# Encoder layer on one core: three of the four late modulation vectors summed on VectorE, ScalarE and GpSimd; Fourier mixer with folded columns

## What is computed

```python
mod = jax.nn.silu(c) @ w_ada[l] + b_ada[l]                    # c: one vector per sequence, w_ada 1024 x 6144
sh_m, sc_m, gt_m, sh_f, sc_f, gt_f = jnp.split(mod, N_MOD, axis=-1)
h = modulate(x, g_mix[l], sh_m, sc_m)
x = x + gt_m[:, None, :] * token_mixer(h, w_in[l], ...)
h = modulate(x, g_ffn[l], sh_f, sc_f)
x = x + gt_f[:, None, :] * expert_choice_moe(h, ...)          # 16 experts, each token list of 128 + 64

# token_mixer: z = h @ w_in, split in zb, zc, za (384 each), zf (256), zu, zv (384 each)
def fourier_mixer(zf):
    f = zf.reshape(b, s, FOURIER_GROUPS, HEAD_DIM)
    y = jnp.real(jnp.fft.fft2(f, axes=(1, 3), norm='ortho'))  # over the sequence and over the head
```

## Time and profile before

| | |
|---|---|
| median of 3 runs | 1515.03 us (1514.19 to 1516.32) |
| the profiled execution's own time | 1515.15 us |
| its span | 1513.3 us |
| TensorE busy (matmuls) | 1436.5 us, 95% |
| VectorE, ScalarE, GpSimd busy | 1032.3, 775.0, 158.1 us |
| mean granted TensorE clock | 0.982 |
| ada steps of the prompt | 72.1 to 271.9 us |
| prompt's sequence transform | 271.9 to 285.8 us |

### The profile page before, as it was taken

The page is one execution under the profiler, slowest core; times in us unless marked ns, Lnnn a source line. Parts: engine busy times, 40 slices in busy tenths (PEclk is TensorE's granted clock), DMA queues, the critical chain, the costliest instruction groups (busy, mean ns, idle before and its releaser), DMA issues.

```text
span 1513.3 us, 22821 instructions
## 1 busy us (share of the span) xinstructions
PE 1436.5 (95%) x8639; PEld 1277.9 (84%) x8639; DVE 1032.3 (68%) x1449; ACT 775.0 (51%) x1020; POOL 158.1 (10%) x129
## 2 busy tenths in 40 slices
PE   2999999999999986999999999999999999999992
PEld 1787777887788866999999999999999999999992
DVE  3422533676769877777777777777777767777776
ACT  4422121523542324666656666666666666666564
POOL 2000000000000002021021021022022022022010
PEclk9999999999999997999999999999999999999996
DMA  9334344554242364687788788788778778778786
GB/s 331 107 113 126 115 150 150 188 180 181 90 120 57 133 240 156 219 275 245 244 265 244 257 257 249 256 260 251 254 245 266 254 243 267 253 241 263 250 280 241
DMA packets 217941, 322.20 MB, mean 213 GB/s; under 512 B 7452, under 2 KB 174440, under 8 KB 217896
## 3 DMA queue, kind: packets, MB, share of 16 engines
q1 hardware_dynamic: 208760, 294.70, 57.8%
q0 software_dynamic: 8064, 26.30, 7.4%
q10 hardware_dynamic: 1072, 0.59, 0.1%
HBM read 290.07 MB, written 31.49 MB: 212 GB/s over the span
## 4 chain that ended last, share of the span: by engine, by line
PE 83%; DVE 8%; ACT 3%; DMA 2%; SPq 1%; issue 1%; POOL 0%; POOLq 0%; DVEq 0%; ACTq 0%
PE ps L1589 25%; PE ps L1237 24%; PE ps L1587 10%; PE ps L1610 4%; PE ps L1602 4%; PE ps L1611 4%; PE ps L1603 4%; PE ps L1606 4%; PE ps L1592 1%; DVE wlo L2172 1%; PE ps L1578 1%; DVE idxu L2040 1%; SPq L631 1%; DVE vals L2038 1%; DVE aff L2041 1%
## 5 line engine op out<-in xcount | busy, mean ns | idle before, releaser
L1589 PE MATMUL ps<-xT,whi 128*128 128x384 f32 x2048 | 576.6, 356 | 1.6 <-DVE xT L2288 1.6
L2172 DVE TENSOR_TENSOR wlo<-raw,whi 128x2048 fp32r<-128x2048 f32 x191 | 435.3, 2292 | 193.1 <-ACT whi L1134 193.1
L1587 PE MATMUL ps<-xT,wlo 128*128 128x192 f32 x1792 | 455.3, 254 | 0.0
L1589 PEld LDWEIGHTS ps<-xT,whi 128*128 128x128 f32 x2048 | 367.9, 189 | 2.4 <-issue 1.9
L1134 ACT ACTIVATE whi<-raw 128x2048 fp32r<-128x2048 f32 x192 | 362.4, 1906 | 0.0
L1587 PEld LDWEIGHTS ps<-xT,wlo 128*128 128x128 f32 x1792 | 342.5, 191 | 0.0
L1237 PE MATMUL ps<-hT,wring 128*128 128x512 f32 x1224 | 289.7, 395 | 5.7 <-DVE hT L1720 5.7
L1237 PEld LDWEIGHTS ps<-hT,wring 128*128 128x128 f32 x1224 | 229.4, 190 | 58.8 <-DVE hT L1720 6.3
L1171 ACT ACTIVATE gu_l<-ps 128x384 f32<-128x384 f32 x128 | 62.9, 491 | 152.4 <-PE ps L1589 152.4
L1237 PE MATMUL ps<-wo,Yhl 128*128 128x512 f32 x576 | 135.5, 393 | 2.4 <-DVE Yhl L1862 1.0
L1237 PEld LDWEIGHTS ps<-wo,Yhl 128*128 128x128 f32 x576 | 106.9, 188 | 25.3 <-issue 2.1
(11 more groups left out here) (236 smaller groups left out, 1551.9 us busy)
## 6 DMA issues: line engine op xcount, KB each, us to landing
raw<-in_w_gate SPq DMA_DIRECT2D x64, 1024.0 KB, 4.8
raw<-in_w_up SPq DMA_DIRECT2D x64, 1024.0 KB, 5.6
raw<-in_w_down SPq DMA_DIRECT2D x64, 1024.0 KB, 5.5
wraw<-in_w_in SPq DMA_DIRECT2D x34, 512.0 KB, 6.0
wraw<-in_w_ada SPq DMA_DIRECT2D x32, 512.0 KB, 4.6
ada_w<-in_w_ada SPq DMA_DIRECT2D x16, 512.0 KB, 11.3
acc_d<-x SPq DMA_DIRECT2D x12, 512.0 KB, 2.7
h_d<-h SPq DMA_DIRECT2D x12, 512.0 KB, 3.9
```

Of the source, the lines that this page charges most:

```text
L1587: pe.matmul(out[:, 0:CAP], wlo[:, slot, w], xT[:, k, 0:CAP], start=False, stop=False, skip_group_check=True)
L1589: mm = pe.matmul(out[:, 0:2 * CAP], whi[:, slot, w], xT[:, k, :], start=k == 0, stop=k == KB - 1, skip_group_check=True)
L2172: dve.tensor_tensor(wlo[:, j % SPL, :], raw[:, j % RAW, :], whi[:, j % SPL, :].bitcast(F32), ALU.subtract).then_inc(w_split, 1)
```

## The change

Four things are changed.

1. **ada parts 0, 1 and 2** (24 of 32 pieces) leave TensorE. For the prompt VectorE forms a running sum, piece times silu(c) per row plus the sum so far (`ada_prompt`). For the sample ScalarE scales the piece into one buffer `ada_part`, and GpSimd adds it to its sum (a copy for the first piece of a part); ScalarE waits for GpSimd before it writes the buffer again. A piece is free when both VectorE and ScalarE are done with it. A new step "sum", one block after a part's last piece, lets TensorE add the 128 partitions of both sums (`ada_sums`, 8 matmuls as wide as those of one ada pair). Part 3 stays as it was.
2. **Fourier columns folded.** VectorE folds the positions n and s-n (`fold`, in the step of zv0), so the head transform needs 16 matmuls of 128 columns (and two of the middle position) in place of 16 (prompt) or 8 (sample) of 256, and the sequence transform half its matmuls and half its constants: two pieces instead of four (prompt), one instead of two (sample). The sums and differences after the head transform go away.
3. The step ab0 comes after zv1 instead of before it, in both sequences.
4. w_out blocks 1 and 2 are loaded behind za2 and zb2. The bias rows of the late parts come one part at a time, because sums and bias lie in space of Y that zb1 and later blocks write.

```diff
-WO_AHEAD = {("zb", 0): 5, ("zb", 1): 6, ("zc", 2): 7}
+AB_JOBS = (2, 1)
+N_SUMMED = (N_ADA - 1) * KB
+WO_AHEAD = {("zb", 0): 5, ("zb", 1): 6, ("zc", 2): 7, ("za", 2): 1, ("zb", 2): 2}
...
-    order = ["zf0", "zf1", "zv0", "ab0", "zv1", "vt0", "zv2", "vt1", "zu0", "vt2", "zu1", "zu2", "zc0", "sv0", "za0", "zb0",
+    order = ["zf0", "zf1", "zv0", "zv1", "ab0", "vt0", "zv2", "vt1", "zu0", "vt2", "zu1", "zu2", "zc0", "sv0", "za0", "zb0",
              "zc1", "za1", "ssq2", "zb1", "zc2", "za2", "zb2"]
...
+        if s or step[0] not in COL:
+            continue
+        blocks += 1
+        if blocks in due:
+            out.append(("sum", due[blocks]))
+        for _ in range(2 if blocks >= len(FIRST) else 0):
+            out.append(("ada", ada))
+            ada += 1
+            if ada % KB == 0 and ada <= N_SUMMED:
+                due[blocks + 1] = ada // KB - 1
...
-            out += [("dft", 0, 0), ("dft", 0, 1), ("dft", 0, 2), ("wo", 0), ("dft", 0, 3)]
-            out += [("wo", b) for b in (1, 2, 3, 4)]
+            out += [("dft", 0, 0), ("dft", 0, 1)] + [("wo", b) for b in (0, 3, 4)]
         else:
-            out += [("dft", 1, m) for m in range(TL[1] // 2)]
+            out.append(("dft", 1, 0))
...
                     elif last[0] == "ada":
-                        if last[1] % KB == KB - 1:
+                        if last[1] < N_SUMMED:
+                            sp.wait_ge(ada_dve, last[1] + 1)
+                            sp.wait_ge(ada_act, last[1] + 1)
+                        elif last[1] % KB == KB - 1:
                             wait_filled(sp, "ada", last[1] // KB)
                         else:
-                            sp.wait_ge(ada_used, last[1] + 1 - last[1] // KB)
+                            sp.wait_ge(ada_used, last[1] + 1 - N_SUMMED)
...
+            for c in range(N_SUMMED):
+                j, k = c // KB, c % KB
+                if j and k == 0:
+                    wait_filled(pool, "ada", j - 1)
+                pool.wait_ge(ada_act, c + 1)
+                if k == 0:
+                    ins = pool.tensor_copy(ada_sum[:, 1, :], ada_part[:, :])
+                else:
+                    pool.wait_ge(ada_pool, c)
+                    ins = pool.tensor_tensor(ada_sum[:, 1, :], ada_sum[:, 1, :], ada_part[:, :], ALU.add)
+                ins.then_inc(ada_pool, 1)
+                if j and k == 0:
+                    mod_rows(j - 1)
+                    bias_row(j)
+            for j in (N_ADA - 2, N_ADA - 1):
+                mod_rows(j)
+                if j < N_ADA - 1:
+                    bias_row(j + 1)
...
+                    if kind == "ada" and i < N_SUMMED:
+                        at_n = raw_n["ada", i]
+                        act.wait_ge(ws_in[at_n % RS], 16 * (at_n // RS + 1))
+                        if i:
+                            act.wait_ge(ada_pool, i)
+                        act.activation(ada_part[:, :], wraw[:, at_n % RS, :], ACT.Copy,
+                                       scale=silc[:, KB + i % KB:KB + i % KB + 1]).then_inc(ada_act, 1)
...
+            def ada_sums(n):
+
+                open_bank("ada", n)
+                pe.wait_ge(ada_dve, KB * (n + 1))
+                pe.wait_ge(ada_pool, KB * (n + 1))
+                pe.wait_ge(pick_ready, 3)
+                for s in range(2):
+                    for j in range(4):
+                        ins = mm(ada_bank("ada", n)[32 * j:32 * (j + 1), :], pick[:, s, :],
+                                 ada_sum[:, s, AW * j:AW * (j + 1)], s == 0, s == 1)
+                fill(ins, "ada", n)
...
-                        for g in range(NG[s]):
-                            wait_drained(pe, "zf", s, 1, g)
-                        for c in range(TL[s] // 2):
-                            par, u = divmod(c, TL[s] // 4)
-                            for half in range(2):
-                                first = par + 2 * P * u + half * (W[s] // 2)
-                                out = open_bank("ab", s, c, half)
-                                for fb in range(2):
-                                    ins = pe.matmul(out[:, 2 * P * fb:2 * P * (fb + 1)],
-                                                    zfT[s][:, fb, first:first + 2 * P - 1:2],
-                                                    chs[:, :, :].rearrange("p a n -> p (a n)"), start=True, stop=True)
-                                fill(ins, "ab", s, c, half)
+                        head_dft(s)
...
+            def head_dft(s):
+
+                quarter, rows = W[s] // 4, W[s] // 8
+                pe.wait_ge(folded, 8 * (s + 1))
+                for par in range(2):
+                    for n in range(AB_JOBS[s]):
+                        out = open_bank("ab", s, par, n)
+                        for q in range(2) if s else (n,):
+                            for ab in range(2):
+                                for fb in range(2):
+                                    first = quarter * (2 * q + ab) + par
+                                    if s:
+                                        cols = slice(P * (2 * q + fb), P * (2 * q + fb + 1))
+                                        at_row = rows * (1 - ab)
+                                    else:
+                                        cols = slice(P * (2 * ab + fb), P * (2 * ab + fb + 1))
+                                        at_row = 0
+                                    more = par == q == 0 and ab == 1
+                                    ins = mm(out[at_row:at_row + rows, cols],
+                                             zfT[s][:, fb, first:first + 2 * rows - 1:2], chs[:, ab, :], True, not more)
+                                    if more:
+                                        ins = mm(out[0:32, cols], middle[:, fb, :], chs[:, 0, :], False, True)
+                        fill(ins, "ab", s, par, n)
...
+            def ada_prompt(c):
+
+                j, k = c // KB, c % KB
+                acc, chunk = ada_sum[:, 0, :], wraw[:, raw_n["ada", c] % RS, :]
+                dve.wait_ge(ws_in[raw_n["ada", c] % RS], 16 * (raw_n["ada", c] // RS + 1))
+                if k == 0:
+                    if j:
+                        wait_filled(dve, "ada", j - 1)
+                    ins = dve.tensor_scalar(acc, chunk, silc[:, k:k + 1], None, ALU.mult)
+                else:
+                    dve.wait_ge(ada_dve, c)
+                    ins = dve.scalar_tensor_tensor(out=acc, in0=chunk, scalar=silc[:, k:k + 1], in1=acc, op0=ALU.mult,
+                                                   op1=ALU.add)
+                ins.then_inc(ada_dve, 1)
...
+            def fold(s):
+
+                half, quarter = W[s] // 2, W[s] // 4
+                sums, differences = halves[s][:, :, 0, :], halves[s][:, :, 1, :]
+                for fb, g in itertools.product(range(2), range(NG[s])):
+                    wait_drained(dve, "zf", s, fb, g)
+                if s == 0:
+                    step(dve.memset(middle[:, :, :], 0.0))
+                step(dve.tensor_tensor(sums, zfT[s][:, :, 0:half], zfT[s][:, :, half:2 * half], ALU.add))
+                step(dve.tensor_tensor(differences, zfT[s][:, :, 0:half], zfT[s][:, :, half:2 * half], ALU.subtract))
+                after_step()
+                for fb in range(2):
+                    four = zfT[s][:, fb, :].rearrange("p (a n) -> p a n", a=4)
+                    near, far = halves[s][:, fb, :, 1:quarter], halves[s][:, fb, :, half - 1:quarter:-1]
+                    dve.tensor_tensor(four[:, 0:4:3, 1:quarter], near, far, ALU.add).then_inc(folded, 1)
+                    dve.tensor_tensor(four[:, 1:3, 1:quarter], near, far, ALU.subtract).then_inc(folded, 1)
+                ends = zfT[s][:, :, :].rearrange("p b (a n) -> p b a n", a=4)
+                dve.tensor_copy(ends[:, :, 0:3:2, 0], halves[s][:, :, :, 0]).then_inc(folded, 1)
+                dve.tensor_copy(ends[:, :, 3, 0], differences[:, :, quarter]).then_inc(folded, 1)
+                dve.memset(ends[:, :, 1, 0], 0.0).then_inc(folded, 1)
+                dve.tensor_copy(middle[:, :, 0], sums[:, :, quarter]).then_inc(folded, 1)
...
-                    both = [AB[s][:, c, q, :, :, :].rearrange("p a b c -> p (a b c)") for q in range(2)]
-                    wait_filled(dve, "ab", s, c, 1)
-                    wait_drained(dve, "ab", s, c, 0)
-                    step(dve.tensor_tensor(both[0], both[1], bank("ab", s, c, 1), ALU.add))
-                    after_step()
-                    drain(dve.tensor_tensor(both[1], both[1], bank("ab", s, c, 1), ALU.subtract), "ab", s, c, 1)
+                for par in range(2) if s == 0 else ():
+                    wait_filled(dve, "ab", s, par, 1)
+                    drain(dve.tensor_copy(AB[s][:, par, 1, :, :, :].rearrange("p a b c -> p (a b c)"),
+                                          bank("ab", s, par, 1)), "ab", s, par, 1)
...
+                            if s == 0 and i == 1:
+                                dve.wait_ge(ada_pool, N_SUMMED)
...
```

(2 more changed lines are left out.)

158 lines of the change are left out of this document (93 added, 65 removed).

## The result

The changed kernel took 1552.25 us (median of 4 runs, 1551.65 to 1557.72) beside 1515.67 us for the kernel before (4 runs on the same chip): ratio 1.0245, with a 95% interval of 1.0225 to 1.0264. It is slower by 37 us. The prediction said 1531, with a range of 1518 to 1543: the sign was right, the size was not, and the time lies above the range. The profiled execution took 1552.09 us, its span is 1550.3 us.

The account below looks back on a forecast made before the run. TensorE was taken to bound the kernel, with 1.8 us of slack in the weight-ring loop. Own time 1515.15 + 11.2 (prompt waits less savings) + 0.3 (w_out group) + 6.1 (clock) - 1.35 (sample) = 1531.4; predicted 1531, range 1518 to 1543.

Parts of the forecast that it names:

- TensorE's savings: Ada pieces -9.0, prompt head transform -2.7 and sequence transform -6.9, sample -1.85 and -0.5: together -20.9 us.
- The ring: Weight-ring slots freed late: second slot 5.5 us after a ScalarE-drained block's last matmuls fill its banks, next weights at 13.4.
- the walk: Queue-by-queue timeline of the prompt from zf1's end at 72.1 us: first w_out tile at 297.0 instead of 285.76.
- the sum of the walk: TensorE's waits before the prompt's first w_out tile: 1.0, 6.4, 2.4, 4.4, 5.7, 5.1 and 4.0 us.
- the clock term: Slower TensorE clock behind the gaps: +6.1 us, at its upper end, with a lower bound of 0.
- The sample term: Sample: -1.85 sequence transform, -0.5 head transform, +1.0 for the fold ahead of a copy the router needs: -1.35 us.
- The walk's end: At the prompt's first w_out tile: 297.0 instead of 285.76, so +11.2 us.
- the 0.3 for the third group of the w_out tile: In the first w_out tile, the third group is held by the last w_out splits: +0.3 us.
- rival 2: GpSimd and VectorE take turns, in the fold, zb0's sums and one convolution: +9, so 1540 us; chance 0.20.
- Its sign: GpSimd's additions at over 3 us each would show that GpSimd and VectorE take turns; the forecast had 2.3.
- Rival 1: Weights after next come in time in ScalarE's blocks and behind za: 1506 us, range 1494 to 1512; chance 0.09.

Follow-up runs that it names:

- the copies: Changed kernel with each of GpSimd's 21 additions replaced by two copies of the scaled piece (sample's three sums left out): 1550.90 us, ratio 1.0227.
- the one at 1498: Changed kernel with loads, drains, pieces and a top-k round reordered, a second scaled-piece buffer and a mended split rule, results whole: 1498.03 us, ratio 0.9878.

## Why the prediction was right and where it was wrong

**TensorE's savings** were right: ada 9.0 as forecast, sequence transform 7.0 (6.9 forecast), head transform 2.0 for 2.7 (4.83 us for the prompt's transform, 4.1 forecast; for the sample's 3.1 as forecast).

**The ring** was the right mechanism. In the block shown, the second slot was free at F + 5.9 (5.5 forecast) and the weights ready at F + 13.6 (13.4 forecast). The waits came where the walk had put them, and moving the loads took 23.6 us away. The step that failed is **the sum of the walk**: its seven terms come to 29.0 us, and 43.5 were measured. The largest part of the gap, by the rows, goes back to the one price that the prediction put at 0, what GpSimd and VectorE do to each other.

| wait | forecast, us | measured, us |
|---|---|---|
| zv1 | 1.0 | 2.0 |
| up to zv2 | 6.4 | 10.9 (4.72 + 6.15) |
| zu1, zu2, zc0 | 2.4 | 2.8 |
| gating | 4.4 | 6.5 |
| zc1 | 5.7 | 6.65 |
| za1 | 5.1 | 6.4 |
| zb1 to zc2 | 4.0 | 8.3 |

Three things stand behind the 14.5 us of difference.

- *VectorE's durations beside GpSimd.* The prediction took the price of this as 0 (its reason, that the clock term was at its upper end, says nothing about the price) and put +9 into a rival. In the changed kernel two of the fold's operations took 2.88 us instead of 0.68 each (rows in the last section), so VectorE was through with the fold 4.4 us later than it could have been, and with the pieces behind it. zv2's weights were issued at 98.55, where the walk had 93, and ScalarE's drains of zv1 and of the head transform stood behind their split. Ahead of the gating the normalisation of v took 4.81 us (2.7 before for the same eight operations). Behind za1 one operation of the convolution took 3.31 us instead of 1.28, ahead of the pieces that free zc2's slots. The waits in question, up to zv2, at the gating and at zc2, are 4.5, 2.1 and 4.3 longer than forecast. The three delays of VectorE that stand in these chains are 4.4, 2.1 and 2.0 us, 8.5 together, an estimate from the rows and close to the rival's 9. The runs don't settle it, since none takes the effect away whole: the copies, which take off two fifths of it, gained 1.3 us with ScalarE's round in place and 6.8 without it (1551.8 to 1545.0).
- *The third sum's bank.* The walk let piece 24 follow the sum at once. But TensorE may open the bank again only when VectorE has drained it, and on VectorE that drain stands behind the splits of w_out 6 and zc2. The run that moved the drain turned 8.3 us of idle time into 7.0 (2.2 and 4.80) and gained nothing, so this wait was missed in the prediction but is not what costs: zc2 would have had to wait for its weights there anyway. They are ready at 274.6 us in the changed kernel, and at 277.2 in that run, which was 1.1 us late at this point and drained the bank first.
- *Landings.* The walk let a w_in load land 3.3 to 5.5 us after the slots before it were free. From its issue to its split the changed kernel's trace has, up to 277 us, between 4.2 (268.04 to 272.26) and 7.2 us (98.55 to 105.71, and 231.04 to 238.26 for za1).

**The clock term** was 6.1, and 9.7 were lost. No run shows the 6.1; the earlier trace rows show 1.5 lost behind one wait, of 2.20 us (4.51 for 3.02). What the traces of the change show in its place is a granted clock of 0.50 behind each of the six waits of 4.7 us and more, and losses of up to 2.3 us for a block behind one (za1, 13.49 for 11.15), 9.7 in all. Of the 9.7 the 1.8 of zc1 lie in front of za1's wait, whose load was issued at 231.04 while zc1 still ran to 234.3; counted with that wait, they leave 7.9 for the clock and make za1's wait 1.8 longer than the table says. Waits between 2.1 and 3.2 us cost about 1.5 and more in some traces and nothing in others (last section).

**The sample term** of -1.35 has the wrong sign: from the first w_out tile to the end the changed kernel lost 0.65 us, though a stretch in the trace of before with a granted clock of 0.50 (394 to 397 us, see the earlier trace rows) was missing there and gave 1.5. That was luck and no effect of the change: the wait of 2.20 us in front of it is the same in both traces. The forecast booked the shorter sequence transform as 1.85 of gain. TensorE waits there for VectorE (3.12 us instead of 0.99) and then runs 18 matmuls in 5.70 instead of 4.34:

```profile
430.26 2.99 PE L1301 MATMUL ps<-hT,wring 128*128 128x512 f32 x12 [2.20 <-DVE hT L1828]
...
538.15 1.95 PE L1301 MATMUL ps<-wraw,AB 128*128 128x128 f32 x16
543.22 5.70 PE L1301 MATMUL ps<-wo,Yhl 128*128 128x512 f32 x18 [3.12 <-DVE Yhl L1999]
```

(The first row is the one that answers to the first of the earlier trace rows.)

Put together: 14.5 (waits) + 3.6 (clock) + 1.2 (lost ahead of 64 us) + 2.0 (sample) + 0.6 (savings, 18.0 for 18.6) = 21.9. The walk's end of +11.2 was 0.8 more than its waits less its savings (29.0 - 18.6), and the 0.3 for the third group of the w_out tile didn't come (332.86 is +36.1 too): 20.8, and the difference between 1531.4 and 1552.1 is 20.7.

**The rivals.** What rival 2 supposed was there, beside the ring, and it gave 1540. Its sign, additions of over 3 us, did not come: GpSimd's additions took 2.52 us on average (one of the 21 took 3.40), and it was mostly VectorE's operations that got longer (2.88 us for 0.68 in the fold). In the steady blocks its price hid behind ScalarE's round; ahead of zv2, of the gating and of zc2 it stood in the chain, as rival 2 had it for the fold and the convolution. Rival 1, the ring keeps up, was wrong for this kernel, and right for the one at 1498: it took eight small edits to make it so.

## What to carry to other kernels

When work is moved from the bounding engine to others that have room, walk each queue and not the totals: who frees the slots, and what stands behind the loads that wait for them. A load that the bounding engine needs belongs ahead of loads whose slots come free late; here that order alone was worth 24 us of the 42 that the sums cost, and with it, a second buffer and some further reorderings the same change went from 2.4% slower to 1.2% faster. And where taking away one suspect shows nothing, take away two before you clear them: two chains of equal length hide each other. Differences of 1 to 2 us belong in the trace and not in the median: one and the same wait of TensorE cost nothing in some kernels here and 1.5 us in others.
